# Samples' scores of cached keys taken head pair by head pair in the attention phases of a fused decoder step

## What is computed

```python
k_past = cache_k[page_table].reshape(8, 512, 16, 64)       # page_table (8, 4)
v_past, logf_past = cache_v[page_table]..., cache_logf[page_table]...
logits = einsum('nqhd,nkhd->nhqk', q, k_all) * 64 ** -0.5
decay = c_q - c_k                                          # c = cumsum(logf_all)
p = softmax(where(causal, logits + decay, -inf))
o = einsum('nhqk,nkhd->nqhd', p, v_all)
y = (o * silu(z)) @ w_out + b_out                          # then a layer norm
```

## Time and profile before

| | us |
|---|---|
| runs (3): median, lowest, highest | 1791.25, 1788.35, 1791.35 |
| profiled execution: its time, its span | 1788.97, 1787.5 |
| PE busy in the span | 1663.9 (93%) |
| DVE busy | 1005.3 (56%) |
| ACT busy | 624.7 (35%) |
| POOL busy | 418.9 (23%) |
| mean granted clock of PE, of full | 0.973 |

### The profile page before, as it was taken

The page is one execution under the profiler, slowest core; times in us unless marked ns, Lnnn a source line. Parts: engine busy times, 40 slices in busy tenths (PEclk is TensorE's granted clock), DMA queues, the critical chain, the costliest instruction groups (busy, mean ns, idle before and its releaser), DMA issues.

```text
span 1787.5 us, 27940 instructions
## 1 busy us (share of the span) xinstructions
PE 1663.9 (93%) x10096; PEld 1438.5 (80%) x10096; DVE 1005.3 (56%) x1568; ACT 624.7 (35%) x980; POOL 418.9 (23%) x432
## 2 busy tenths in 40 slices
PE   6999989999999988999869999999999999977975
PEld 4899989999999988999757878777777778756742
DVE  2433253334343346225556686867677776889875
ACT  2222122111121226225433636455454646361121
POOL 0000011111011000002122624344352625254221
PEclk9999999999999998999989999999999999988997
DMA  8111112212222212234223122111212120248767
GB/s 357 36 47 35 47 60 95 83 59 93 82 78 74 89 53 89 93 99 148 94 72 118 37 92 61 59 59 59 82 59 65 53 82 36 73 144 271 263 244 298
DMA packets 50191, 180.45 MB, mean 101 GB/s; under 512 B 6522, under 2 KB 8186, under 8 KB 48850
## 3 DMA queue, kind: packets, MB, share of 16 engines
q1 hardware_dynamic: 31650, 116.11, 19.1%
q0 software_dynamic: 18480, 63.53, 9.9%
HBM read 154.07 MB, written 17.15 MB: 96 GB/s over the span
## 4 chain that ended last, share of the span: by engine, by line
PE 75%; DVE 10%; issue 5%; ACT 3%; DMA 3%; POOL 2%; POOLq 1%; SPq 0%; DVEq 0%; ACTq 0%
PE bank L1684 20%; PE bank L1685 19%; PE bank L1686 19%; PE bank L2046 2%; PE bank L2000 2%; PE bank L2048 2%; PE bank L2047 2%; PE bank L1819 2%; PE bank L2028 1%; PE bank L2027 1%; DVE bank L1383 1%; DMA fsw<-units 1%; POOL p_lo L533 1%; PE bank L1799 1%; DVE pages L1366 1%
## 5 line engine op out<-in xcount | busy, mean ns | idle before, releaser
L1684 PE MATMUL bank<-h_hi,w_lo 128*128 128x344 f32 x1152 | 374.8, 325 | 8.1 <-DVE h_lo L1076 6.9
L1685 PE MATMUL bank<-h_lo,w_hi 128*128 128x344 f32 x1152 | 369.0, 320 | 0.0
L1686 PE MATMUL bank<-h_hi,w_hi 128*128 128x344 f32 x1152 | 368.7, 320 | 0.0
L533 POOL TENSOR_TENSOR p_lo<-parg,p_hi 128x512 fp32r<-128x512 f32 (+1 forms) x192 | 213.9, 1131 | 170.4 <-ACT p_hi L919 170.0
L1684 PE MATMUL bank<-x_hi,w_lo 128*128 128x512 f32 x528 | 222.8, 422 | 10.9 <-POOL x_lo L485 5.4
L1684 PEld LDWEIGHTS bank<-h_hi,w_lo 128*128 128x128 f32 x1152 | 217.7, 189 | 13.5 <-issue 10.5
L1685 PEld LDWEIGHTS bank<-h_lo,w_hi 128*128 128x128 f32 x1152 | 217.8, 189 | 0.2 <-issue 0.2
L1686 PEld LDWEIGHTS bank<-h_hi,w_hi 128*128 128x128 f32 x1152 | 217.7, 189 | 0.0
L1685 PE MATMUL bank<-x_lo,w_hi 128*128 128x512 f32 x528 | 210.6, 399 | 0.0
L1686 PE MATMUL bank<-x_hi,w_hi 128*128 128x512 f32 x528 | 210.4, 399 | 0.0
L1684 PE MATMUL bank<-y_hi,w_lo 128*128 128x320 f32 (+2 forms) x512 | 180.0, 352 | 30.4 <-DVE w_lo L1034 18.9
(11 more groups left out here) (301 smaller groups left out, 2643.6 us busy)
## 6 DMA issues: line engine op xcount, KB each, us to landing
raw<-units SPq DMA_DIRECT2D x121, 512.0 KB, 3.3
ada_ring<-w_ada SPq DMA_DIRECT2D x32, 512.0 KB, 3.3
pages<-cache_k POOLq DMA_DIRECT2D x32, 512.0 KB, 5.3
pages<-cache_v POOLq DMA_DIRECT2D x32, 512.0 KB, 6.9
ada_first<-w_ada SPq DMA_DIRECT2D x8, 1024.0 KB, 15.9
ckb<-scr_c POOLq DMA_DIRECT2D x16, 512.0 KB, 4.1
KX<-KA SPq DMA_DIRECT2D x32, 256.0 KB, 4.3
xT<-x_t SPq DMA_DIRECT2D x2, 2064.0 KB, 23.1
```

The source lines that it names most:

```text
L533: g.tensor_tensor(p_lo[:, r, off:HALF], parg[:, r, off:HALF], p_hi[:, r, off:HALF].bitcast(F32), ALU.subtract).then_inc(S("p_ready"), 1)
L1684: mm(out, lhs_lo, rhs_hi, start=first, stop=False)
L1685: mm(out, lhs_hi, rhs_lo, start=False, stop=False)
L1686: return mm(out, lhs_hi, rhs_hi, start=False, stop=last)
```

## The change

In phases 0 to 5, DVE multiplies (`score_mul`) and sums (`score_sum`) four chunks of keys per phase: of every page only the 128 columns of the phase's two heads, two samples (eight pages) at a time, in one buffer `kpb`. SP stores the two heads' q (`put_q`), loads it back as a broadcast (`get_q`), reads page numbers and loads the chunks (`load_keys`), each chunk behind the sum of the one before, and stores the scores (`put_scores`). The heads of phases 6 and 7 are scored from `kp2` by eight `score_late`, two in phase 7, three behind it, three in the projection. SP also loads `fpg` and `fsw`, which POOL did. `by_key` lays q, stored feature by feature with the eight samples side by side, against the keys.

The samples' softmax, their value pages (two buffers instead of four) and products move into the last projection (behind halves n = 1 to 15), and the steps behind it lie between the final norm's tiles. `turn(1, 0)`, its copy and the early scores leave phase 7. `scr_q` is now laid out by head pair; the page table's load counts on `ws_in`.

```diff
+        kpb = at("kpb", [P, 2, NP, P], F32, R1 + 6 * 4096)
+        qb = at("qb", [P, P, NS], F32, R1 + 7 * 4096)
+        kp2 = at("kp2", [P, NS * NP, 2 * P], F32, R2)
+        qb2 = [at("qb20", [P, P, NS], F32, R3 + 36864), at("qb21", [P, P, NS], F32, R3 + 12288)]
+        sct = at("sct", [P, KB, NS, NP, 2], F32, R3 + 43008)
...
+            def put_q(j):
+                sp.wait_ge(S("ev_s"), 4 * j + 2)
+                settle(sp, S("settled"))
+                sp.dma_start(scr_q[bass.ds(j, 1), :, :].rearrange("a p n -> p (a n)"), kqvzS[:, 1, j, 0:NS]).then_inc(S("scr_q"), 16)
+            def get_q(j, dst):
+                sp.dma_start(dst[:, :, :].rearrange("p f n -> p (f n)"),
+                             scr_q[bass.ds(j, 1), :, :].rearrange("a p n -> a (p n)").broadcast_to([P, P * NS])).then_inc(S("qb_in"), 16)
+            def page_of(b, p):
+                return sp.value_load(ptab[0:1, b * NP + p:b * NP + p + 1], min_val=0, max_val=cache_k.shape[0] - 1)
...
+            def load_keys(j, c):
+                wait(sp, S("pages_used"), 4 * j + c)
+                settle(sp, S("settled"))
+                for b in range(2):
+                    for p in range(NP):
+                        page = page_of(2 * c + b, p)
+                        sp.dma_start(kpb[:, b, p, :], cache_k[bass.ds(page, 1), :, bass.ds(j * P, P)].rearrange("a p c -> p (a c)"))\
+                          .then_inc(S("kp_in"), 16)
+            def load_phase(j):
+                load_swapped(j)
+                if not isinstance(j, int):
+                    put_scores(j - 1)
+                put_q(j)
+                sp.wait_ge(S("scr_q"), 16 * j + 16)
+                wait(sp, S("qk_prod"), 4 * j)
+                settle(sp, S("settled"))
+                get_q(j, qb)
+                for q in range(4):
+                    load_b(j + 1, q)
+                    load_keys(j, q)
...
+            sp.wait_ge(S("ws_in"), 48)
+            sp.wait_ge(S("ln1_back"), TT)
+            load_phase(0)
+            with sp.Fori(1, LATE) as j:
+                load_phase(j)
+            load_swapped(LATE)
+            put_scores(LATE - 1)
+            for q in range(4):
+                load_b(LATE + 1, q)
+            load_swapped(KB - 1)
+            for j in range(LATE, KB):
+                put_q(j)
             sp.wait_ge(S("mm"), 12 * KB - 5)
             load(U_FA, U_FA % 2)
             sp.wait_ge(S("mm"), 12 * KB - 2)
             load(U_FA + 1, (U_FA + 1) % 2)
-            load_swapped(KB - 1)
+            sp.wait_ge(S("nl_ready"), 16 * KB)
+            sp.wait_ge(S("vt_done"), KB)
+            sp.wait_ge(S("v_out"), 16 * KB)
+            sp.wait_ge(S("scr_q"), 16 * KB)
+            for j in range(LATE, KB):
+                get_q(j, qb2[j - LATE])
+            sp.wait_ge(S("sc_out"), 16 * LATE)
+            sp.dma_start(sct[:, 0:LATE, :, :, :].rearrange("p j b a h -> p j (b a h)"), scr_s[:, :, :].rearrange("j p c -> p j c"))\
+              .then_inc(S("late_in"), 16)
+            sp.wait_ge(S("mm"), 12 * KB)
+            for b in range(NS):
+                for p in range(NP):
+                    page = page_of(b, p)
+                    sp.dma_start(kp2[:, b * NP + p, :], cache_k[bass.ds(page, 1), :, LATE * P:KB * P].rearrange("a p c -> p (a c)"))\
+                      .then_inc(S("kp_in" if b < NS // 2 else "late_in"), 16)
+            for b in range(NS):
+                for p in range(NP):
+                    page = page_of(b, p)
+                    sp.dma_start(fpg[:, p, b, :], cache_f[bass.ds(page, 1), :, :].rearrange("a p h -> p (a h)")).then_inc(S("fpg_in"), 16)
...
+            sp.wait_ge(S("pages_used"), SCORED + NS)
+            for b in range(KB):
+                sp.dma_start(fsw[:, b, :, :], units[U_FA - WB + b, :, :, :]).then_inc(S("fsw_in"), 16)
...
-            load_f(0)
-            load_f(1)
-            with pool.Fori(1, NS // 2) as i:
-                for s in range(2):
-                    load_q(2 * i + s, s)
-                    pool.wait_ge(S("pages_used"), 2 * i + s - 1)
-                    load_set(cache_k, 2 * i + s, s)
-                    load_f(2 * i + s)
...
-            pool.wait_ge(S("r2_ready"), 2 * KB)
-            pool.wait_ge(S("lo_ready"), U_FS)
-            for b in range(KB):
-                pool.dma_start(fsw[:, b, :, :], units[U_FA - WB + b, :, :, :]).then_inc(S(f"fsw_in{b // 4}"), 16)
+            for n in range(NS):
+                pool.wait_ge(S("pages_used"), SCORED - 4 if n == 0 else SCORED + max(n - 1, 0))
+                load_values(n, n % 2)
...
+            def by_key(q, c):
+                return q[:, :, 2 * c:2 * c + 2].rearrange("p (o f) b -> p b o f", o=1).broadcast_to([P, 2, NP, P])
+            def score_mul(j, c):
+                dve.wait_ge(S("kp_in"), 16 * 2 * NP * (4 * j + c + 1))
+                if c == 0:
+                    dve.wait_ge(S("qb_in"), 16 * j + 16)
+                settle(dve, S("settled"))
+                v.tensor_tensor(kpb[:, :, :, :], kpb[:, :, :, :], by_key(qb, c), ALU.mult).then_inc(S("qk_prod"), 1)
...
+            def score_late(m):
+                c, jj = divmod(m, 2)
+                n = 4 * LATE + m
+                keys = kp2[:, 2 * NP * c:2 * NP * (c + 1), jj * P:(jj + 1) * P]
+                if m == 0:
+                    dve.wait_ge(S("qb_in"), 16 * KB)
+                if m == 0:
+                    dve.wait_ge(S("kp_in"), 16 * NP * (NS * LATE + NS // 2))
+                if m == 4:
+                    dve.wait_ge(S("late_in"), 16 + 16 * NP * NS // 2)
+                v.tensor_tensor(keys.rearrange("p (b a) f -> p b a f", a=NP), keys.rearrange("p (b a) f -> p b a f", a=NP),
+                                by_key(qb2[jj], c), ALU.mult).then_inc(S("qk_prod"), 1)
                 dve.wait_ge(S("qk_prod"), n + 1)
-                last = v.tensor_reduce(scol[:, p, b, :], pages[:, b % 2, p, :].rearrange("p (h d) -> p h d", d=HD), AX.X, ALU.add)
-                if p == NP - 1:
-                    last.then_inc(S("pages_used"), 1)
-            EARLY = 8
+                if m == 0:
+                    dve.wait_ge(S("nl_ready"), 16 * KB)
+                v.tensor_reduce(sct[:, LATE + jj, 2 * c:2 * c + 2, :, :].rearrange("p b a h -> p (b a) h"),
+                                keys.rearrange("p n (h d) -> p n h d", d=HD), AX.X, ALU.add).then_inc(S("pages_used"), 1)
...
                 peak(j, 4)
                 peak(j, 5)
+                if keys:
+                    score_mul(j, 0)
                 take_samples(j, 3)
                 split_lo(j + 1, 0)
+                if keys:
+                    score_sum(j, 0)
...
                 z_evac(j, 1)
+                if keys:
+                    score_mul(j, 1)
                 exponents(j, 3)
...
                 invert(j, 0, 0)
+                if keys:
+                    score_sum(j, 1)
                 exponents(j, 6)
...
                 exponents(j, 8)
+                if keys:
+                    score_mul(j, 2)
                 if more:
                     evac_s(j + 1, 1)
                     split_lo(j + 1, 2)
                 else:
-                    score(0)
+                    score_late(0)
                 exponents(j, 9)
+                if keys:
+                    score_sum(j, 2)
                 if not more:
-                    score(1)
+                    score_late(1)
                 exponents(j, 10)
                 if not more:
-                    score(2)
                     y2_low(0)
                     y2_low(1)
                 exponents(j, 11)
                 if more:
                     kq_low(j + 1, 0)
+                    if keys:
+                        score_mul(j, 3)
+                        score_sum(j, 3)
...
+                    if n == 0:
+                        score_late(5)
+                    if n == 1:
+                        tok(1, qtok, 2)
+                        tok(2, ktok, 3)
+                    if n == 2:
+                        score_late(6)
+                        tok(3, vtok, 2)
+                    if n == 3:
+                        score_late(7)
                         new_key()
+                        gather_scores()
+                    if n == 4:
+                        decay()
+                        logits()
+                    if n == 5:
+                        weights()
+                    if n == 6:
+                        spread_weights()
+                    if n == 7:
+                        gate_s()
                     if n == 14:
+                        mask_o()
+                    if n == 15:
+                        gated_s()
...
+            layer_norm_stats(0, TT)
+            layer_norm_stats(1, TT)
...
+            finish(0)
+            layer_norm_stats(2, TT)
...
+            norm_sum(rS[:, :, :], KB)
+            finish(1)
+            layer_norm_stats(3, TT)
+            norm_square(3, rS[:, :, :], KB, rS[:, :, :])
+            finish(2)
+            layer_norm_stats(4, TT)
```

(105 more changed lines are left out.)

253 lines of the change are left out of this document (98 added, 155 removed).

## The result

The changed kernel takes **1826.77 us** (median of four runs, 1825.06 to 1828.96), against 1791.3 for the kernel before in the same series: 1.0207 times as long, 95% interval 1.0187 to 1.0227. The forecast was 1795 with a range of 1783 to 1812. The profiled execution took 1828.96 with a span of 1827.4; before, the span was 1787.5, so the traces differ by 39.9 where the medians differ by 35.5. One of the four executions of `e2_fixed_pages` further down was slow throughout (2430.96 us at a granted clock of 0.617) and is left out of its median.

A forecast was written before the change was run, and what follows sets the result against it. TensorE's order of work was taken to bound the phases; phases 0 to 5 +12.4, start of block 2 0, block 2 to the projection's end +9.7, tail -18.9, small waits +0.5 gave +3.7, 1795 us, range 1783 to 1812.

The forecast's parts named there:

- The bound: In the phases TensorE's order of work limits; whatever delays an operand it takes just in time costs again each phase.
- Slot 0: Product ahead of take_samples(j, 3), sum ahead of peak(j, 6): 2.28 us into 1.52 of VectorE idling, +0.76 per phase.
- Slots 1 and 2: Pairs behind z_evac/invert and behind exponents(j, 8) and (j, 9) fit VectorE's waits for scores: 0 for TensorE.
- GpSimd's side: VectorE's two-input products and GpSimd's p_lo hinder each other; priced only as 0.6 us delay of slot 2's sum.
- Slot 3: Pair behind kq_low(j+1, 0) waits for the fourth key chunk, pages 1.0 us each on SP: +1.3 per phase.
- The rival of the strided product: Reading q with a 32-byte step makes products 2.3 us instead of 1.2: +17, 1812 us; chance 0.06.
- The rival of SP: At 1.15 us a page SP becomes the bound: phases +19.6, block 2 12 us later, +23, 1814 us; chance 0.13.
- The rival of early keys: A page costs SP 0.75 us or less, slot 3 is free, xb2 11 us earlier: -4, 1787 us; chance 0.25.
- Block 2 to the end: From block 2's start to the projection's end, with the samples' steps and value products inside: 91.4 us, +9.7.
- Rival 4: Two-buffered value loads starve the projection, each product waiting 1.5 us: +9 more, 1804 us; chance 0.11.
- The tail: Behind the projection, final norm tiles with sample steps between, the serial 25 us gone: 52.6 us, -18.9.

The follow-up runs named there:

- e2_fixed_pages: Changed kernel with SP's page numbers as constants, so no register reads (other pages are scored than the table names): 1802.98 us, 1.0077 of the kernel before.
- e4: Changed kernel with no scores in phases 0 to 5 (no product, sum, page, q or score moved there): 1781.05 us, 0.9943 of the kernel before.
- e5: Changed kernel with q read side by side and only the first chunk of keys loaded, all products still made: 1792.50 us, 1.0015 of the kernel before.
- e1: Changed kernel with products reading q side by side instead of with a 32-byte step (wrong pairing of q and keys): 1803.35 us, 1.0077 of the kernel before.
- e3: Changed kernel with only the first chunk of keys loaded, all 24 products and sums still made: 1813.85 us, 1.0136 of the kernel before.
- f2: Changed kernel with q stored sample by sample, that store ahead of KX's copy, and 16 of 32 page numbers held in registers: 1777.92 us, 0.9930 of before.
- e6: Changed kernel with 16 of 32 page numbers read once and held in SP's registers, nothing left out: 1804.15 us, 1.0075 of the kernel before.
- f3: f2 with VectorE's fourth product started only when GpSimd's last p_lo is done: 1778.66 us, 0.9934 of the kernel before.

## Why the prediction was wrong, point by point

**The bound** was read rightly: TensorE's order, in which what delays an operand costs the same in each phase. Six phases gave 42.0, and without scores they gave 0 (e4).

**Slot 0**: forecast +0.76, measured +1.6. The step that failed is the duration, 1.21 taken from a contiguous product for one that reads q with a step. With the right length, 0.76 and 0.9 more, the working gives 1.7. With products of 1.22 (e5) the slot cost 0.64: the mechanism was right and the length was not.

**Slots 1 and 2**: forecast 0, measured +1.0, of which 0.7 is one wait for `p_lo`: GpSimd's pair beside the product of slot 2 took 5.04 instead of 3.54. This too is the length: with products of 1.22 these slots cost nothing (48.39 in e5 and 48.38 to 48.42 in e1), as forecast.

**GpSimd's side.** I had written down that such operations hinder each other and then counted only VectorE's side of it. GpSimd's side is the one that TensorE waits for, and it costs even at the assumed length, in slot 3: +0.97 a phase in e5, 5.8 us in all, which the forecast put at nothing.

**Slot 3**: forecast +1.3, measured +3.55. The mechanism is the one forecast, and the time between is almost exact: the third sum ended 4.8 us ahead of the half `kq_low`, forecast 4.7. Then two terms were too small: from that sum's end to the fourth product's start 11.0 us passed, forecast 9.7 (pages 1.16 apart instead of 1.0, and 0.9 ahead of the first issue), and the product was 1.06 longer. 1.3 and these two are 3.7. What the forecast lacks is the price of a stall of 3.2 us on TensorE beyond itself, 1.2 us of slow matmuls, though matmuls of 0.79 behind a wait were in the rows of the projection.

By cause, from the square of e1, e3 and e5: 9.6 us for the pairs at their assumed length (forecast 4.6, slot 0 alone), 19.4 to 20.2 for the step, 12.2 to 13.0 for the late keys (forecast 7.8).

**The rival of the strided product** had a chance of 0.06 and a price of 2.3 us a product, +17 in all. The length was confirmed (2.15 to 2.49), and the price came out a little higher (19.4 to 20.2); the chance was wrong. I argued against it from reductions with a step, 1.1 ns per further element. They read 64 and 128 elements and have one input; the difference of two such short ones (0.07 us over 64) says nothing firm on a second operand of a two-input product over 1024. The Trainium skill, *SBUF — State Buffer*, section Door 1: The DMA port swizzle, states a penalty for crossing to a new 16-byte line; with a step of 32 bytes each element crosses. e1 agrees: 1.23 us against 2.27, which is 1.0 ns more an element. I had cited it and weighed a poor row above it. No run reads with a step of 8 or 16 bytes, so whether it is the new line or any step that costs is not shown.

**The rival of SP** was priced at a page of 1.15 and a start of block 2 12 us later. Measured are 1.12 to 1.16 and +11.1. The prediction took 0.6 for the register read, which was right (e2: 1.12 less 0.50), but 0.33 for the issue, which is one instruction's length; from one issue to the next it is 0.50 even with constant pages. GpSimd's two numbers, 0.54 and 0.63, would have given 1.17.

**The rival of early keys** was added up wrongly. Its terms, +4.6 in the phases, -4.5 at the start and the rest as in the forecast (+9.7, -18.9, +0.5), give -8.6 and 1783, not -4 and 1787, and 1783 is the lower end of the whole range. Nor do the chances divide it: "faster" has 0.25, which is all of this rival, though the text splits it. The nearest run is f2, with the keys in time and products of 1.2: 12.1 us below the kernel before of its series.

**Block 2 to the end**: forecast 91.4, measured 94.1. The two-buffered value loads cost what was said: product 2 waited 3.21 (3 forecast), product 7 0.77 (1 in all). Rival 4 didn't come.

**The tail**: forecast 52.6, measured 49.2. From phase 6 on, the change is a gain once SP's queue is out of the way: 330.0 us in e6 and 328.3 in f2 against 344.9.

**The size in all.** The forecast counted one mechanism at a time, as rivals that exclude each other. The strided product and the slow page are independent and both held: 17 and 19 on top of the forecast's 4 are 40, against 35.5 measured (39.9 in the traces). That the sum comes so near is partly luck: GpSimd's side (5.8) and the part behind block 2 (3.4) were missing, and they are balanced by late keys at 12 to 13 where that rival has 15, a start of -3.0 without a cause and a tail 4.0 shorter than forecast. A range that let two of them hold together would have held the time.

## What to carry to other kernels

A new instruction's duration is that of its access pattern, not of its element count: take the row from one with the same steps and the same number of inputs, and where there is none, give both lengths real weight. Where a single queue does address work, count issue, register read and offset, each from a row, and multiply by all that stands ahead of what the critical engine needs. When two rivals don't exclude each other, add them up together as well. And when a wait is removed, look at what runs beside the work that moves into its place: here a late product had spared GpSimd, and the early one held it up.

## What was not expected of the hardware

Holding 16 of 32 page numbers in SP's registers took the issue from 1.16 to (3.93 - 0.33)/7 = 0.51 us a page. A store of 4 KB in pieces of 4 bytes took 8.9 to 10.3 us to be seen as done, in pieces of 32 bytes 1.6. Of a VectorE product and a GpSimd operation that met, the one that began second became longer, by most of what was left of the other: GpSimd's pair went from 1.42 to 3.25 beside a product of 2.22 (e3) and to 2.39 beside one of 1.37 (f2), and the product from 1.22 to 2.72 behind the start of GpSimd's `w_sc` (f3), while `w_sc` kept its 1.90. Why the clock falls behind some waits of 1.7 us and not behind others, in e3 in two phases of six, stays open.
